# Latent attention heads of a diffusion backbone: other steps for the inverse of the sums, the projections and the sums, V beside the first maxima, and a rounded matmul for the maxima's row

## The reference

```python
q = (rms_norm(p[8], gq) @ w_uq).reshape(B, T, MLA_HEADS, MLA_NOPE + MLA_ROPE)
kv = (rms_norm(p[9], gkv) @ w_ukv).reshape(B, T, MLA_HEADS, MLA_NOPE + MLA_V)
k_nope, v = kv[..., :MLA_NOPE], kv[..., MLA_NOPE:]
k_rope = jnp.broadcast_to(p[10][:, :, None, :], (B, T, MLA_HEADS, MLA_ROPE))
q = rms_norm(q, qk_gain[0])
k = rms_norm(jnp.concatenate([k_nope, k_rope], axis=-1), qk_gain[1])
# then a rotation of the last 32 columns of q and k (latent tokens only)
s = jnp.einsum('bqhd,bkhd->bhqk', q, k) * scale
p = jax.nn.softmax(s, axis=-1)
o = jnp.einsum('bhqk,bkhd->bqhd', p, v)
```

## Time and profile before

| | |
|---|---|
| profiled execution | 2629.88 us, its span 2628.1 us |
| median of three runs | 2633.29 us |
| TensorE matmul busy | 2240.8 us, 85% |
| VectorE, ScalarE, GpSimd busy | 972.9, 771.3, 613.3 us |
| latent heads, layer 0 | 604.2 to 855.5 us |
| latent heads, layer 1 | 2003.9 to 2215.7 us |
| rounding of a weight unit (L467) | 1059 ns, 204 times |
| quarter of a unit's rest (L441) | 783 ns, 816 times |

### The profile page before, as it was taken

One profiled execution on the slowest core, in us unless ns is written; L12 is line 12 of the kernel. 1 busy time (PEld: TensorE's weight loads), 2 busy tenths in 40 slices (PEclk: granted clock), 3 DMA queues, 4 the chain that ended last, 5 costly groups with the idle time before them and its releaser, 6 DMA issues.

```text
span 2628.1 us, 29125 instructions
## 1 busy us (share of the span) xinstructions
PE 2240.8 (85%) x11572; PEld 1784.5 (68%) x11572; DVE 972.9 (37%) x1670; ACT 771.3 (29%) x1282; POOL 613.3 (23%) x820
## 2 busy tenths in 40 slices
PE   5777999586887799999999967798776887899998
PEld 4467866475665588788878855686555655688886
DVE  3457401616666511111101265550434664321211
ACT  3233222023666311111111133322113664322221
POOL 0110300020000233333333320031021101455555
PEclk8899965698898799999999979996588998999999
DMA  6200124010000124132323210020011000232322
GB/s 243 89 17 12 52 89 136 8 52 23 8 8 9 56 97 128 57 120 97 104 74 127 81 43 17 17 64 32 0 42 32 17 9 16 80 96 92 97 92 96
DMA packets 76732, 166.22 MB, mean 63 GB/s; under 512 B 5296, under 2 KB 47024, under 8 KB 75584
## 3 DMA queue, kind: packets, MB, share of 16 engines
q1 hardware_dynamic: 75648, 163.15, 19.0%
q10 hardware_dynamic: 960, 1.31, 0.2%
HBM read 162.33 MB, written 2.10 MB: 63 GB/s over the span
## 4 chain that ended last, share of the span: by engine, by line
PE 73%; DVE 12%; ACT 7%; issue 5%; DMA 1%; POOL 1%; DVEq 0%; SPq 0%; ACTq 0%; POOLq 0%
PE psum L887 19%; PE psum L888 18%; PE psum L889 18%; PE psum L1141 2%; PE psum L932 2%; PE psum L1166 2%; DMA wm<-w_mod 1%; PE psum L942 1%; PE psum L1129 1%; PE psum L1324 1%; DVE naptlo L1635 1%; PE psum L1184 1%; PE psum L1195 1%; PE psum L1039 1%; DVE n_t L1544 1%
## 5 line engine op out<-in xcount | busy, mean ns | idle before, releaser
L441 POOL TENSOR_TENSOR wlo<-raw,whi 128x256 fp32r<-128x256 f32 x816 | 613.1, 783 | 2002.0 <-ACT whi L467 2002.0
L887 PE MATMUL psum<-hhi,whi 128*128 128x512 f32 (+1 forms) x1640 | 586.5, 358 | 44.5 <-DVEq L1482 14.6
L888 PE MATMUL psum<-hlo,whi 128*128 128x512 f32 (+1 forms) x1640 | 581.1, 354 | 0.0
L889 PE MATMUL psum<-hhi,wlo 128*128 128x512 f32 (+1 forms) x1640 | 580.5, 354 | 0.0
L467 ACT ACTIVATE whi<-raw 128x1024 fp32r<-128x1024 f32 x204 | 215.2, 1059 | 1058.6 <-PE psum L889 1058.4
L887 PEld LDWEIGHTS psum<-hhi,whi 128*128 128x128 f32 x1640 | 313.8, 191 | 101.3 <-issue 21.4
L889 PEld LDWEIGHTS psum<-hhi,wlo 128*128 128x128 f32 x1640 | 313.7, 191 | 42.5
L888 PEld LDWEIGHTS psum<-hlo,whi 128*128 128x128 f32 x1640 | 314.4, 192 | 40.4
L1983 DVE TENSOR_TENSOR ffuf<-ffsa,psum 128x768 f32<-128x768 f32 (+1 forms) x44 | 36.1, 821 | 534.5 <-ACT ffsa L836 534.5
L887 PE MATMUL psum<-uhi,whi 128*128 128x512 f32 (+1 forms) x528 | 191.0, 362 | 8.3 <-POOL wlo L441 7.5
L888 PE MATMUL psum<-ulo,whi 128*128 128x512 f32 (+1 forms) x528 | 189.7, 359 | 0.0
(11 more groups left out here) (280 smaller groups left out, 3476.2 us busy)
## 6 DMA issues: line engine op xcount, KB each, us to landing
raw<-w_stream SPq DMA_DIRECT2D x204, 512.0 KB, 3.5
wm<-w_mod SPq DMA_DIRECT2D x80, 512.0 KB, 4.7
wm<-w_mod SPq DMA_DIRECT2D x8, 1024.0 KB, 17.7
xres<-x_t SPq DMA_DIRECT2D x8, 384.0 KB, 5.4
out<-xres SPq DMA_DIRECT2D x8, 256.0 KB, 2.9
mlsel<-c_gate ACTq DMA_DIRECT2D x2, 216.0 KB
consts<-c_f SPq DMA_DIRECT2D x1, 353.0 KB, 7.2
marope<-c_rope ACTq DMA_DIRECT2D x4, 64.0 KB
```

The lines of the kernel that those rows point to most:

```text
L441: ins = nc.gpsimd.tensor_tensor(wlo[:, q % 2, c:c + UW // 4], raw[:, q % RAW, c:c + UW // 4], whi[:, q % 2, c:c + UW // 4], ALU.subtract)
L887: mm(dst, ah, bh, start=first, stop=False)
L888: mm(dst, ah, bl, start=False, stop=False)
L889: return mm(dst, al, bh, start=False, stop=last)
```

## The change

The lists are written in another order, with the ring's order to match:

- ScalarE: `q_rsqrt` of head h + 2 stands in the last step of round h, ahead of the row; before, in step 0 of the next round. `q_square` stands in step 5 ahead of `k_rsqrt`; before, in step 4. `inverse` for the latent queries stands in step 1 in layer 0, and in step 2 ahead of `q_round` in layer 1; before, in step 2 behind `q_round`. Roundings of weight units (`his`) stand at other steps.
- TensorE: `k_project` is split, the latent columns in step 2 and the context columns in step 3; `q_project` is in step 4 in place of 3; `q_sums` of head h + 2 is in the last step, before in step 0 of the next round; both first pairs of context maxima stand in step 3 behind the values, the column maxima two in step 4 and two in step 5, the last context maxima in step 6.
- V's tiles (`v_tile`, `v_hi`, `v_lo`) are in round -1, beside the maxima of head 0, in place of round -2; the ones beside V are written there too. The first unit of head weights changes places with V's.
- `max_row` is a rounded (fp32r) matmul with a rounded identity, from rounded maxima, into row 0 of its bank in place of row 96.
- The context queries' output has semaphores and functions of its own (`inverse_context`, `o_scale_context`, `o_round_context`, `o_rest_context`), without the two drains.

The core of the diff:

```diff
-MA_CQ, MA_KR, MA_CKV, MA_V, MA_HEAD, MA_OUT = 19, 22, 23, 25, 26, 30
+MA_CQ, MA_KR, MA_CKV, MA_V, MA_OUT = 19, 22, 23, 26, 30
+MA_HEAD = (25, 27, 28, 29)
...
-                    if nxt2 and h % 2 == 0 and h >= 0:
-                        his(u0(l, MA_HEAD) + (h + 2) // 2 + 2)
-                    if h == MLA_HEADS - 2:
-                        his(u0(l, MA_OUT) + 2)
                     for i in range(n):
                         if now:
                             probs(h, i)
-                        if h == -2 and i < TT:
+                        if i == 0 and nxt:
+                            k_round(h + 1)
+                        if i == 0 and h in (1, 3, 6):
+                            his(u0(l, {1: MA_HEAD[2], 3: MA_HEAD[3], 6: MA_OUT + 1}[h]) + 1)
+                        if i == (1 if full else 2) and was:
+                            inverse(h - 1)
+                        if i == 2 and nxt:
+                            q_round(h + 1)
+                        if i == 2 and was and full:
+                            inverse_context(h - 1)
+                        if i == 3 and nxt2:
+                            k_square(h + 2)
+                        if i == 3 and was:
+                            o_round(h - 1)
+                        if i == 4 and was and full:
+                            o_round_context(h - 1)
+                        if i == 5 and nxt2:
+                            q_square(h + 2)
+                            k_rsqrt(h + 2)
+                        if h == -1 and i < TT:
                             v_hi(i)
-                            if i == TT - 1:
-                                his(u0(l, MA_HEAD) + 2)
-                        if i == 0 and nxt:
-                            q_rsqrt(h + 1)
-                            k_round(h + 1)
-                        if i == 2:
-                            if nxt:
-                                q_round(h + 1)
-                            if was:
-                                inverse(h - 1, 0)
-                                if full:
-                                    inverse(h - 1, 1)
-                        if i == 3:
-                            if nxt2:
-                                k_square(h + 2)
-                            if was:
-                                o_round(h - 1, 0)
-                        if i == 4:
-                            if nxt2:
-                                q_square(h + 2)
-                            if was and full:
-                                o_round(h - 1, 1)
-                        if i == 5 and nxt2:
-                            k_rsqrt(h + 2)
+                        if h == -1 and i == n - 1:
+                            his(u0(l, MA_HEAD[1]) + 1)
+                        if i == n - 1 and nxt2:
+                            q_rsqrt(h + 2)
                         if i == n - 1 and nxt:
...
-                def k_project(h):
-                    wh, wl = unit(u0(l, MA_HEAD) + h // 2)
+                def k_project(h, r0, r1):
+                    wh, wl = unit(u0(l, MA_HEAD[h // 2]))
                     if G(h):
-                        pe.wait_ge(k_t, G(h))
-                    for r0, r1 in ranges(True):
-                        if r0 == 0 and G(h):
-                            pe.wait_ge(q_t, G(h))
-                        for k in range(2):
-                            c = 512 * (h % 2) + 384 + 64 * k
-                            ins = mm3(K_PS[0:64, r0:r1], wh[:, c:c + 64], wl[:, c:c + 64],
-                                      MA["ckhi"][:, k, r0:r1], MA["cklo"][:, k, r0:r1], k == 0, k == 1)
-                    ins.then_inc(k_proj, 1)
+                        pe.wait_ge(q_t if r0 == 0 else k_t, G(h))
+                    for k in range(2):
+                        c = 512 * (h % 2) + 384 + 64 * k
+                        ins = mm3(K_PS[0:64, r0:r1], wh[:, c:c + 64], wl[:, c:c + 64],
+                                  MA["ckhi"][:, k, r0:r1], MA["cklo"][:, k, r0:r1], k == 0, k == 1)
+                    if r0 == 0:
+                        ins.then_inc(k_proj, 1)
 
                 def q_project(h):
-                    wh, wl = unit(u0(l, MA_HEAD) + h // 2)
...
-                    pe.wait_ge(col_max, (2 * G(h) if full else MLA_HEADS * (DEPTH - 1) + G(h)) + x + 1)
+                    if x == 0:
+                        pe.wait_ge(col_max, G(h) + 1)
+                    else:
+                        at = RINGS[l, "ctx", h, 2]
+                        pe.wait_ge(bank_free[at % 4], at // 4 + 1)
                     for t in range(2 if x else 4):
-                        c = 12 + t if x else 8 + t
-                        ins = mm(dst[96:97, P * t:P * t + P], MA["mx"][:, c:c + 1], ident, start=True, stop=True)
+                        c = 4 + t if x else t
+                        ins = mm(dst[0:1, P * t:P * t + P], MA["mn"][:, c:c + 1], identr[:, :], start=True, stop=True)
                     ins.then_inc(bank_full[b], 1)
 
...
-                        if h == -2 and i < TT:
+                        if i == 2 and nxt2:
+                            k_project(h + 2, CTX_LEN, TOK)
+                        if i == 3 and nxt2:
+                            k_project(h + 2, 0, CTX_LEN)
+                        if i == 4 and nxt:
+                            max_scores(h + 1, 0)
+                            max_scores(h + 1, 1)
+                        if i == 4 and nxt2:
+                            q_project(h + 2)
+                        if i == 5 and nxt:
+                            max_scores(h + 1, 2)
+                            max_scores(h + 1, 3)
+                        if i == 6 and nxt:
+                            max_context(h + 1, 2)
+                        back = lat_back(l, h, i, 2)
+                        if back is not None and back[0] < MLA_HEADS:
+                            values(*back)
+                        if i == 3 and nxt:
+                            max_context(h + 1, 0)
+                            max_context(h + 1, 1)
+                        if i == 4 and nxt2:
+                            k_sums(h + 2)
+                        if i == n - 1 and nxt2:
+                            q_sums(h + 2)
+                        if h == -1 and i < TT:
                             v_tile(i)
                             if i == TT - 1:
                                 pe.drain().then_inc(w_used, 1)
-                        if nxt and i == 0:
-                            q_sums(h + 1)
-                        if nxt2 and i == 2:
-                            k_project(h + 2)
-                        if nxt and i in (2, 3):
-                            max_context(h + 1, i - 2)
-                        if nxt and i == 3:
-                            max_scores(h + 1, 0)
-                        if nxt2 and i == 3:
-                            q_project(h + 2)
-                        if nxt and i == 4:
-                            max_scores(h + 1, 1)
-                            max_scores(h + 1, 2)
-                        if nxt and i == 5:
-                            max_scores(h + 1, 3)
-                            if full:
-                                max_context(h + 1, 2)
-                        if nxt2 and i == 4:
-                            k_sums(h + 2)
-                        back = lat_back(l, h, i, 2)
-                        if back is not None and back[0] < MLA_HEADS:
-                            values(*back)
-                        if nxt and i == n - 1:
+                        if i == n - 1 and nxt:
...
+                        if i == 2 and was:
+                            o_scale(h - 1)
+                        if i == 2 and nxt:
+                            k_rest(h + 1)
+                            q_rest(h + 1)
+                        if i == 3 and was and full:
+                            o_scale_context(h - 1)
+                        if i == 3 and nxt:
+                            max_c(h + 1, 0)
+                            max_c(h + 1, 1)
+                        if i == 4 and nxt:
+                            max_x(h + 1, 0)
+                            max_x(h + 1, 1)
                         if i == 5 and nxt:
                             max_x(h + 1, 2)
                             max_x(h + 1, 3)
                             max_both(h + 1)
-                            if full:
-                                max_c(h + 1, 2)
-                                V.drain().then_inc(col_max, 1)
+                        if i == 6 and nxt:
+                            max_c(h + 1, 2)
+                        if i == 4 and was:
+                            o_rest(h - 1)
+                        if i == 5 and was and full:
+                            o_rest_context(h - 1)
                         if now:
                             probs_lo(h, i)
+                        if h == -1 and i < TT:
+                            if i == 0:
+                                v_ones_set()
+                            v_lo(i)
```

(36 more changed lines are left out.)

131 lines of the change are left out of this document (62 added, 69 removed).

## The result

The changed kernel takes 2647.89 us (median of six runs, 2645.5 to 2650.99) against 2631.49 for the kernel before (2625.8 to 2636.77, six runs): a ratio of 1.0065, interval 1.0051 to 1.0079. It is slower, as forecast, by 16.4 us where 10 were forecast; 2647.9 lies inside the range 2616 to 2658. The profiled execution took 2649.45 us.

A forecast was written before the change was run, and what follows sets the result against it. TensorE was taken to bound the kernel. Layer 0's -1.1 and layer 1's +10.85 gave +9.8 us on 2629.88, 2639.7; with the runs' median 3.4 above that execution, 2643 us, range 2616 to 2658.

The forecast's parts named there:

- Start of a head: Latent heads: first values at +7.2 us in place of +10.35 in layer 0, +6.95 in place of +9.03 in layer 1.
- The units' roundings: Rounding of head weight units: rounded a head before use, the units' other order costing or giving at most 0.1 us, taken 0.
- End of a head: Fourth maxima wait for K's logarithm, next scores for the row; full-clock period +0.5 us in layer 0, +1.65 in layer 1.
- Clock: Heads 1 to 5: clock falls keep costing 1.94 us a head in layer 0 and 1.44 in layer 1.
- a rival with 0.11: More falls: one more half-clock stretch a head, about 1.5 us net on ten heads, +15, 2658 us; chance 0.11.
- the prediction's own sign: Latent stretches: forecast is wrong in size if the clock's share moves by more than 0.05.
- Before the first scores: Stretch before the first head: first scores 1.5 us later in layer 0, 1.1 later in layer 1; bounds -3 and +5 each.
- The other heads: Layer 0: head 0 -1, head 6 -2.4, head 7 -1.7 us; layer 1: head 0 +1.5, heads 6 and 7 0.
- The rounded row: Maxima's row before next scores: saving worth nothing while its copy waits behind q's exponential, otherwise at most 0.9 us a head.
- hidden tail: Rival: head-end waits vanish and only gains stay, 2605 us, half hidden 2620; chance whole or half 0.18.
- Its deciding point: Head's end on ScalarE: for the faster rival, K's logarithm must start before the sixth scores.

The follow-up runs named there:

- e8: Kernel before, with the inverse of the latent queries' sums a step earlier in layer 0 and ahead of q's rounding in layer 1: 2602.97 us, 0.9903.
- e10: Changed kernel with the inverse of the latent queries' sums back behind q's rounding in step 2: 2669.65 us, 1.0145.
- e1: Changed kernel with q's squares and K's inverse root ahead of the sixth probabilities on ScalarE: 2606.86 us, 0.9915.
- e9: Changed kernel with only q's squares back in step 4, K's inverse root still behind the sixth probabilities: 2627.10 us, 0.9993.
- e5: Changed kernel with eight more passes of the third column maxima for heads 1 to 7 of each layer: 2637.01 us, 1.0032.
- e4: Changed kernel with V's tiles, their rounding and the ones back in the round before: 2643.92 us, 1.0062.
- e7: Kernel before, with the rounded row of maxima alone: 2631.15 us, 1.0015.
- e3: Changed kernel with q's squares and K's root ahead of the sixth probabilities, and the row ahead of q's sums and root: 2600.01 us, 0.9894.
- e12: Kernel before, with K's inverse root ahead of the sixth probabilities and the latent inverse moved earlier: 2583.58 us, 0.9825.

## Why the prediction was right, and where its sizes were off

*Start of a head.* Forecast +7.2 and +6.95, measured +7.45 and +8.54. The terms given for layer 0 (q ready at +5.9, a rest of 0.65, the scaling with its signal 0.84) in fact add to +7.4. It is right in layer 0, and e8 and e10 show that the earlier inverse is what brought it. The trace shows that VectorE's list is then last, as forecast: the inverse ends at 764.20, and the scaling of the output starts at 765.77 without idle time. In layer 1 this step of the prediction failed: there the inverse, behind the third probabilities, is still last (also in heads 2 and 5), and the scores for them ran partly at half clock.

```profile
763.57 0.63 ACT L775 ACTIVATE marec<-marec 64x512 f32<-64x512 f32 x1
765.77 0.69 DVE L1928 TENSOR_TENSOR maof<-psum,marec 64x512 f32<-64x512 f32 x1
2147.08 0.69 DVE L1928 TENSOR_TENSOR maof<-psum,marec 64x512 f32<-64x512 f32 x1 [1.41 <-ACT marec L775]
```

*The units' roundings*, taken at 0, are not free. In rounds 1, 3 and 6 they stand in step 0, and GpSimd makes the unit's rest while VectorE works on the rotation. The same instruction on VectorE in layer 0's head 3, with GpSimd at work, and in head 4, without:

```profile
732.56 1.14 DVE L1855 TENSOR_TENSOR mar<-mar,marope 32x512 f32<-32x512 f32 x1
731.92 4.64 POOL L443 TENSOR_TENSOR wlo<-raw,whi 128x256 fp32r<-128x256 f32 x4 [53.66 <-ACT whi L469]
763.62 0.68 DVE L1855 TENSOR_TENSOR mar<-mar,marope 32x512 f32<-32x512 f32 x1
```

Three such instructions take 1.3 us more in all, and the first values of heads 1 and 3 come at +8.92 and +9.04 in place of +7.45 (0.3 to 0.4 us of that is the scores at half clock). No run moves the roundings alone, so what they cost the whole kernel is not shown.

*End of a head.* The release at the fourth maxima was forecast at +20.9 and came at +20.51; in layer 1 at +19.4 and +20.37, where the first values had come late. The cause named, K's logarithm behind probabilities and squares, is shown by e1 and e9. From the release to the next scores I had 6.5 and 4.2 us. Layer 1 shows 2164.00 - 2159.75 = 4.25. Layer 0's head 1 shows 6.48:

```profile
691.36 0.50 PE L1337 MATMUL psum<-makhi,maqhi 96*128 96x512 f32 x1 [2.20 <-ACT mar L742]
697.84 0.47 PE L893 MATMUL psum<-maqhi,makhi 97*128 97x512 f32 x1 [1.99 <-ACT maqhi L767]
```

but head 4, with the clock at 0.66 there, 9.38. Order and durations were right; the clock was the term mis-sized.

*Clock.* I kept today's loss per head (1.94 and 1.44 us) and put more falls into a rival with 0.11. At the upper level the forecast periods were 27.4 and 23.55; measured 29.6 and 25.5. If all of the difference is the clock's, layer 0 kept its loss (2.2) and layer 1 went to 1.95; the late first values above are in these numbers too. By the prediction's own sign (a move of the granted clock by more than 0.05) it was wrong in size in layer 1, where the clock moved by 0.07. The row of the Trainium skill that I weighed ("TensorE: Matmul & The Clock Gate", section "Why this matters for your kernels"), by which such gaps would not lower the clock, fails again: in heads 1 to 5 of layer 1 the granted clock is 0.86, and the waits there (in all, times, longest) are

```profile
PE psum L893 <- ACT maqhi L767: 11.0, 6, 2.0
PE psum L1337 <- ACT mar L742: 10.2, 5, 2.1
PE psum L893 <- DVE maof L1928: 9.5, 5, 2.0
```

None is over 2.2 us, and the filling of one (e5) raised the clock.

*Before the first scores.* The rotated q was forecast near 622.3 and TensorE's wait for it ended at 623.31 in a stage that began 1.1 us later. The first scores came at 37.7 us after the stage's start against 36.1, +1.7 for a forecast +1.5. In layer 1 +0.4 for +1.1.

```profile
605.36 0.66 PE L893 MATMUL psum<-ckhi,whi 128*64 128x512 f32 x1 [14.68 <-DVEq L1490]
623.31 0.30 PE L893 MATMUL psum<-ckhi,whi 128*64 128x256 f32 x1 [2.94 <-DVE mar L1856]
635.32 0.49 PE L1337 MATMUL psum<-makhi,maqhi 96*128 96x512 f32 x1 [1.78 <-ACT mar L742]
643.09 0.47 PE L893 MATMUL psum<-maqhi,makhi 97*128 97x512 f32 x1 [1.94 <-ACT maqhi L767]
```

e4 shows that this is not V's move: with V back it is 37.3. The second long chain, with the same logarithm, is what is left. With the squares back a step (e9) the wait for the logarithm there is 1.10 us in place of 1.78 and the first scores come after 35.6; in layer 1 they come after 34.5, as without.

*The other heads.* Layer 0: head 0 +0.4 (forecast -1), heads 6 and 7 together -6.1 (-4.1). Layer 1: head 0 +2.35 (+1.5), head 6 +1.1, head 7 and the tail +2.5 (both 0). The last two missed by 3.6 us together, heads 1 to 5 by 1.5 in layer 0 and 2.5 in layer 1. In head 6 of layer 1 the row waited 2.11 us for the last maxima, 0.79 before; the new order has two of them in the last of six steps. In head 7 nothing was moved, but the granted clock was 0.72 against 0.82 before. Sum by the stages: layer 0 0.0 for -1.1, layer 1 +17.1 for +10.85.

*Where luck came in.* Direction and cause were right. That the total lies within 5 us of the forecast is partly luck: the last head of layer 0 gave 4.1 us where 1.7 were forecast, and the last head of layer 1 lost 2.5 where nothing was; the granted clock there went from 0.84 to 0.90 and from 0.82 to 0.72, and the two misses cancel. What is left is a loss forecast too small in the heads before them.

*The rounded row.* Valued at nothing while q's root stands ahead of its copy. The matmuls did shrink:

```profile
L1360 PE MATMUL psum<-identr,maneg x80: 220/223/1095, 640.4 to 2209.6; 128*1 128x128 f32 x80
L1354 PE MATMUL psum<-consts,mamax x160: 269/272/417, 638.5 to 2194.0; 128*1 128x128 f32 x160
```

80 of them in place of the 160 of the kernel before (second line; ns, least, median, most). e7 shows that it gives nothing even where the root is not ahead, which I had not claimed: I expected 0.5 to 0.9 us a head there.

*The rivals.* The hidden tail was priced at 2605; made true in half by e1 (priced at 2620) and whole by e3 it is 2607 and 2600. Its deciding point, K's logarithm before the sixth scores' exponentials, is the edit of e1.

## What to carry to other kernels

When an engine works through a fixed list, look for an instruction whose inputs have long been ready and which frees a buffer, but which stands behind one that waits for TensorE's own next product. Moving it ahead gave some 40 us here and 20 on the kernel before. Judge a reordering by its last step as well as its first: what is taken from a head's start and put into its end only moves the wait. And count idle time of TensorE at more than its length, since the clock behind it is part of the price: 1.9 of 4.3 us a head in layer 0, 1.4 of 2.9 in layer 1.

## What was not expected of the hardware

More matmul work made the program faster: 112 extra matmuls inside waits took 6 to 11 us off. And the two edits of e12 together kept the clock at 1.00 through heads 1 to 5 of both layers where it had been 0.91 and 0.93. So 46 us came off (a ratio of 0.9825) for waits that add up to less in the profile before: 28.6 us for the scaled output and K's logarithm, 14.4 over heads 0 to 6 of layer 0 and 14.2 over those of layer 1:

```profile
PE psum L887 <- DVE maof L1917: 9.0, 6, 1.6
PE psum L1354 <- ACT mar L737: 5.2, 6, 1.0
```

And an instruction of VectorE took 1.14 us in place of 0.68 while GpSimd was at work.
